# Half of the layer-0 column moves on ScalarE's queue, and two mixer blocks of layer 1 turned by VectorE instead of TensorE

## The reference, cut to what matters

```python
for layer in range(DEPTH):                       # DEPTH = 2
    xn = rmsnorm(h, tok_norm_g[layer])
    if layer % 2 == 0:
        mix, q_mem = deltanet_mixer(...)
    else:
        mix, q_mem = spatial_gating_mixer(...)   # u * sg, 1536 wide
    mo = memory_attention(q_mem, mem_n, w_kv)
    h = h + concatenate([mix, mo]) @ tok_w_out[layer]
    hn = rmsnorm(h, ffn_norm_g[layer])
    h = h + square(relu(hn @ ffn_w1[layer])) @ ffn_w2[layer]
return rmsnorm(h, final_norm_g)
```

## Time and profile before

| | us |
|---|---|
| median of 3 runs | 2287.87 |
| lowest, highest | 2287.43, 2288.89 |
| the profiled execution | 2289.45 |
| its span in the profile | 2287.1 |
| busy time of PE in it | 2267.3 |

### The profile page before, as it was taken

The page is one execution under the profiler, slowest core; times in us unless marked ns, Lnnn a source line. Parts: engine busy times, 40 slices in busy tenths (PEclk is TensorE's granted clock), DMA queues, the critical chain, the costliest instruction groups (busy, mean ns, idle before and its releaser), DMA issues.

```text
span 2287.1 us, 33236 instructions
## 1 busy us (share of the span) xinstructions
PE 2267.3 (99%) x10565; PEld 1889.2 (83%) x10565; DVE 1446.8 (63%) x2465; ACT 1267.9 (55%) x2303; POOL 360.5 (16%) x698
## 2 busy tenths in 40 slices
PE   9999999999999999999999999999999999999997
PEld 7888888888888888888888888888888888888886
DVE  6678788787766555555655655566555555566554
ACT  6566475574456544455554555546565444556544
POOL 0010100000332410013421100021233000242100
PEclk9999999999999999999999999999999999999999
DMA  9655365464577766677766675667777666777665
GB/s 335 182 157 161 114 168 139 137 186 117 172 209 213 219 204 194 195 203 220 218 209 206 203 218 157 167 206 222 211 220 216 198 193 195 212 220 211 204 194 158
DMA packets 253035, 443.84 MB, mean 194 GB/s; under 512 B 38124, under 2 KB 40045, under 8 KB 252781
## 3 DMA queue, kind: packets, MB, share of 16 engines
q1 hardware_dynamic: 231709, 420.15, 62.7%
q0 software_dynamic: 20480, 21.01, 2.8%
q10 hardware_dynamic: 720, 1.06, 0.1%
HBM read 419.00 MB, written 2.10 MB: 184 GB/s over the span
## 4 chain that ended last, share of the span: by engine, by line
PE 93%; DVE 3%; ACT 1%; DMA 1%; issue 1%; POOL 1%; SPq 0%; POOLq 0%; ACTq 0%; DVEq 0%
PE pair L566 29%; PE pair L568 29%; PE pair L567 29%; PE aux L766 3%; PE aux L577 2%; DVE w_lo L1601 1%; DVE r L1946 1%; PE aux L813 0%; DMA raw<-in_dn_w_in 0%; POOL xn_late L2427 0%; DVE attnT L1940 0%; DVE projections L1846 0%; ACT r L1323 0%; PE aux L697 0%; PE aux L714 0%
## 5 line engine op out<-in xcount | busy, mean ns | idle before, releaser
L1601 DVE TENSOR_TENSOR w_lo<-raw,w_hi 128x512 fp32r<-128x512 f32 x1536 | 1025.2, 692 | 640.4 <-ACT w_hi L1064 636.9
L1064 ACT ACTIVATE w_hi<-raw 128x512 fp32r<-128x512 f32 x1536 | 945.7, 633 | 803.4 <-DMA raw<-in_ffn_w 630.4
L566 PE MATMUL pair<-w_hi,xT 128*128 128x512 f32 x1984 | 781.6, 394 | 4.2 <-DVE w_lo L1601 1.9
L568 PE MATMUL pair<-w_hi,xT 128*128 128x512 f32 x1984 | 772.9, 390 | 0.0
L567 PE MATMUL pair<-w_lo,xT 128*128 128x512 f32 x1984 | 772.4, 389 | 0.0
L566 PEld LDWEIGHTS pair<-w_hi,xT 128*128 128x128 f32 x1984 | 372.6, 188 | 84.2 <-issue 3.4
L568 PEld LDWEIGHTS pair<-w_hi,xT 128*128 128x128 f32 x1984 | 372.4, 188 | 78.4
L567 PEld LDWEIGHTS pair<-w_lo,xT 128*128 128x128 f32 x1984 | 372.8, 188 | 74.6
L566 PE MATMUL pair<-w_hi,hid_hi 128*128 128x512 f32 x1012 | 393.8, 389 | 0.1
L568 PE MATMUL pair<-w_hi,hid_lo 128*128 128x512 f32 x1012 | 393.7, 389 | 0.0
L567 PE MATMUL pair<-w_lo,hid_hi 128*128 128x512 f32 x1012 | 393.7, 389 | 0.0
(11 more groups left out here) (255 smaller groups left out, 1164.6 us busy)
## 6 DMA issues: line engine op xcount, KB each, us to landing
raw<-in_ffn_w SPq DMA_DIRECT2D x1024, 256.0 KB, 3.2
raw<-in_dn_w_in SPq DMA_DIRECT2D x208, 256.0 KB, 2.9
raw<-in_tok_w_out SPq DMA_DIRECT2D x128, 256.0 KB, 3.2
raw<-in_gm_w_in SPq DMA_DIRECT2D x112, 256.0 KB, 2.9
xn_late<-xn_late POOLq DMA_DIRECT2D x640, 32.0 KB, 3.0
raw<-in_mem_w_kv SPq DMA_DIRECT2D x64, 256.0 KB, 3.3
r<-in_mem_columns SPq DMA_DIRECT2D x8, 256.0 KB, 5.4
h<-in_x_columns SPq DMA_DIRECT2D x8, 256.0 KB, 5.6
```

Of the source, the lines that this page charges most:

```text
L566: pe.matmul(acc, act_hi[:, kt, tokens], w_hi[:, slot], start=start, stop=False)
L568: mm = pe.matmul(acc, act_lo[:, kt, tokens], w_hi[:, slot], start=False, stop=last and k == 1)
L1064: act.activation(w_hi[:, slot], raw[:, slot], ACT.Copy).then_inc(hi_ready, 1)
L1601: dve.tensor_tensor(w_lo[:, slot], raw[:, slot], w_hi[:, slot].bitcast(F32), ALU.subtract).then_inc(tiles_split, 1)
```

## The change

In layer 0 the 16 transfers of each of the two blocks are shared out: POOL issues those of two rows of squares, ACT those of the other two, from its own queue. ACT has them in `refill` at steps 2 (block 0) and 4 (block 1), each behind a wait for DVE's turning of that block. Pairs 0 to 3 then wait for both halves.

In layer 1 blocks 0 and 1 of `mix` go the second way: DVE turns each right behind its gating (`turn_mix`), POOL issues the 2 x 16 transfers (`move_mixed`), and ACT and DVE read from `xn_late`. PE transposes pairs 4 and 5 alone. In the plan, pairs 2 and 3 stand at steps 6 and 7 instead of 3 and 4.

```diff
-A_FN1 = A_MIX1 + 6
+A_FN1 = A_MIX1 + 2
-MIX_REFILL = ((), (0,), (1,), (2,), (3,), (), (), (), (), (4,), (5,))
+MIX_REFILL = ((), (0,), (1,), (), (), (), (2,), (3,), (), (4,), (5,))
+        turned_mix = lambda n: flat_late[:, 1024 * n:1024 * n + 1024]
+        moved_mix = lambda n: flat_late[:, 1024 * n + 2048:1024 * n + 3072]
+        def move_columns(e, r, n, squares, landed):
+            e.wait_ge(sem("columns_turned"), 2 * sum(MOVED[0:r]) + 2 * n + 2)
+            turned = turned_at(r, n).rearrange("p (a m y) -> p a m y", a=4, m=2)
+            moved = moved_at(r, n).rearrange("p (m b y) -> p b m y", m=2, b=4)
+            for a in squares:
+                for b in range(4):
+                    e.dma_start(moved[32 * a:32 * a + 32, b], turned[32 * b:32 * b + 32, a]
+                                ).then_inc(landed, 16)
...
             def mix_refill(plan):
                 for pairs in plan:
                     for p in pairs:
-                        pe.wait_ge(sem("gated"), 2 * (p // 2) + 2)
-                        pair_transposes(mix_fill[1][p], mix, p)
+                        if p > 3:
+                            pe.wait_ge(sem("gated"), 2 * (p // 2) + 2)
+                            pair_transposes(mix_fill[1][p], mix, p)
             def out_block(n):
                 for s in range(SLABS):
-                    if s < 6:
+                    if s < 4:
+                        pe.wait_ge(sem("mix_split"), s + 1)
+                    elif s < 6:
                         drained(pe, mix_fill[1][s])
...
             def refill(r, gain, plan, ends, slab=None):          # ScalarE
-                for pairs in plan:
+                for step, pairs in enumerate(plan):
+                    if r == 0 and step in (2, 4):
+                        move_columns(act, r, step // 2 - 1, (2, 3), sem(f"columns_moved_too{step // 2 - 1}"))
...
-                            act.wait_ge(sem(f"columns_moved{r}{p // 2}"), 256)
+                            act.wait_ge(sem(f"columns_moved{r}{p // 2}"), 256 if r else 128)
+                            if r == 0:
+                                act.wait_ge(sem(f"columns_moved_too{p // 2}"), 128)
...
                 for pairs in MIX_REFILL[0:8]:                    # ScalarE, out_split
                     for p in pairs:
-                        operand_hi(A_MIX1 + p, p, None)
+                        act.wait_ge(sem(f"mix_moved{p // 2}"), 256)
+                        slab_done(act, 8 * (B_GM + 6) + p)
+                        act.activation(by_square(xT_hi[:, 2 * p:2 * p + 2, :]), mixed_columns(p), ACT.Copy
+                                       ).then_inc(sem("xT_hi_ready"), 2)
...
+            def turn_mix(n):                                     # VectorE
+                for m in range(2):
+                    dve.wait_ge(sem("gated"), 2 * n + m + 1)
+                    dve.transpose(turned_mix(n)..., mix[:, m, n * NB:(n + 1) * NB]...
+                                  ).then_inc(sem("mix_turned"), 1)
             def gating(b):
                 yield
                 gate(b)
+                turn_mix(b)
                 yield
             def out_split():
                 for step, pairs in enumerate(MIX_REFILL):
                     if step == 1:
                         gate(1)
+                        turn_mix(1)
...
                     for p in pairs:
-                        operand_lo(A_MIX1 + p, p, None, 80 + 2 * (p + 1) + 4 * (p > 3))
+                        if p > 3:
+                            operand_lo(mix_fill[1][p], p, None, 84 + 2 * (p + 1))
+                        else:
+                            dve.wait_ge(sem("xT_hi_ready"), 80 + 2 * (p + 1))
+                            high, low = (by_square(x[:, 2 * p:2 * p + 2, :]) for x in (xT_hi, xT_lo))
+                            dve.tensor_tensor(low, mixed_columns(p), high.bitcast(F32), ALU.subtract).then_inc(sem("mix_split"), 1)
...
+            def move_blocks(r):                                  # GpSimd
+                for n in range(MOVED[r]):
+                    move_columns(pool, r, n, range(2 if r == 0 else 4), sem(f"columns_moved{r}{n}"))
+            def move_mixed():
+                for n in range(2):
+                    pool.wait_ge(sem("mix_turned"), 2 * n + 2)
+                    ...                                          # 16 transfers, as in move_columns
-            move_columns(0)
+            move_blocks(0)
             norm(N_FFN0)
             move_hidden(0)
-            move_columns(1)
+            move_blocks(1)
             norm(N_TOK1)
             norm(N_V, MIX)
-            move_columns(2)
+            move_mixed()
+            move_blocks(2)
```

More of the change, by code:

```diff
@@ L326, in encoder_trunk @@
         mix_fill = [[A_MIX0, A_MIX0 + 1, A_MIX0A, A_MIX0A + 1, A_MIX0B, A_MIX0B + 1],
-                    [A_MIX1 + p for p in range(6)]]
+                    {4: A_MIX1, 5: A_MIX1 + 1}]
         refill_slots = [{p: a + p - 2 * n for p in range(2 * n, 8)} for a, n in zip((A_FN0, A_TN1, A_FN1), MOVED)]
@@ L369, in columns_moved, with mixed_columns, by_square @@
             return moved_at(r, p // 2).rearrange("p (x f i) -> p f x i", x=8, f=4)[:, 2 * (p % 2):2 * (p % 2) + 2]
+        def move_columns(e, r, n, squares, landed):
[6 more added lines that the diff above has]
+                                ).then_inc(landed, 16)
+        def mixed_columns(p):
+            return moved_mix(p // 2).rearrange("p (x f i) -> p f x i", x=8, f=4)[:, 2 * (p % 2):2 * (p % 2) + 2]
+        def by_square(t):
+            return t.rearrange("p k (x i) -> p k x i", x=8)
         def freed(ins, n):
@@ L1563, in out_split @@
                     for p in pairs:
-                        operand_hi(A_MIX1 + p, p, None)
+                        operand_hi(mix_fill[1][p], p, None)
                     yield
@@ L2293, in gate @@
                     dve.tensor_tensor(t, t, ug[:, m, b * NB:(b + 1) * NB], ALU.mult).then_inc(sem("gated"), 1)
+            def turn_mix(n):
+                for m in range(2):
+                    dve.wait_ge(sem("gated"), 2 * n + m + 1)
+                    dve.transpose(turned_mix(n).rearrange("p (a m f i) -> p m f a i", a=4, m=2, f=4)[:, m],
+                                  mix[:, m, n * NB:(n + 1) * NB].rearrange("p (f a i) -> p f a i", f=4, a=4)
+                                  ).then_inc(sem("mix_turned"), 1)
             def gating(b):
@@ L2417, in move_hidden @@
                                                    ).then_inc(sem(f"hidden_moved{half}{j}"), 16)
-            def move_columns(r):
+            def move_blocks(r):
                 for n in range(MOVED[r]):
-                    pool.wait_ge(sem("columns_turned"), 2 * sum(MOVED[0:r]) + 2 * n + 2)
-                    turned = turned_at(r, n).rearrange("p (a m y) -> p a m y", a=4, m=2)
-                    moved = moved_at(r, n).rearrange("p (m b y) -> p b m y", m=2, b=4)
+                    move_columns(pool, r, n, range(2 if r == 0 else 4), sem(f"columns_moved{r}{n}"))
+            def move_mixed():
+                for n in range(2):
+                    pool.wait_ge(sem("mix_turned"), 2 * n + 2)
+                    turned = turned_mix(n).rearrange("p (a m y) -> p a m y", a=4, m=2)
+                    moved = moved_mix(n).rearrange("p (m b y) -> p b m y", m=2, b=4)
                     for a in range(4):
@@ L2427, in move_columns @@
                             pool.dma_start(moved[32 * a:32 * a + 32, b], turned[32 * b:32 * b + 32, a]
-                                           ).then_inc(sem(f"columns_moved{r}{n}"), 16)
-            move_columns(0)
+                                           ).then_inc(sem(f"mix_moved{n}"), 16)
+            move_blocks(0)
             norm(N_FFN0)
             move_hidden(0)
-            move_columns(1)
+            move_blocks(1)
             norm(N_TOK1)
             norm(N_V, MIX)
-            move_columns(2)
+            move_mixed()
+            move_blocks(2)
             norm(N_FFN1)
```

## The result

| | before | changed |
|---|---|---|
| median of 18 runs, us | 2287.88 | 2292.0 |
| the profiled execution | 2289.45 | 2291.4 |
| its span | 2287.1 | 2289.6 |

The ratio is 1.0018, with a 95% interval of 1.0011 to 1.0026: 4.1 us slower, 2.5 to 6.0 by the interval. The two profiled executions differ by less, 2.5 us in the span, because that of before lay 1.6 us above its median and that of the changed kernel 0.6 us under its own.

What follows compares the result with a forecast made beforehand. TensorE was taken as the bound, busy 2267.3 of 2287.1 us at top clock. Layer 1's -1.92 and layer 0's +0.42 made -1.5 us, median 2287.87 to 2286.4 us, range 2284.1 to 2288.8.

Steps and rivals of the forecast that it cites:

- c: Layer 0: time from one transfer issue to the next on ScalarE's queue, taken as 0.41 us, between 0.38 and 0.47.
- What the new issues cost: Layer 0 part of the prediction: ScalarE's two runs of eight issues delay the FFN's start to 619.07 us, losing 0.42 us.
- -1.92 - 6.14: Fixed terms of the forecast total for both layers, -1.92 - 6.14 + 16c us; above zero from c = 0.504.
- the formula 612.51 + 16c: Layer 0: time in us at which TensorE's FFN starts, after VectorE's pair 0; 619.07 with c = 0.41, against 618.65 before.
- issue is dear, and the kernel is slower: Rival, chance 0.10: ScalarE between slabs 4 and 7 of `PART_B`; with c at 0.62 the total is +1.9 us, 2289.7 us.
- Slab 7's wait: Layer 0: TensorE would start slab 7 at 613.70 us but get it at 615.3, a new wait of 1.6 us.
- The same recurrence: Layer 0: step-by-step times of ScalarE's issues and splits and VectorE's 0.6 us slots, leading to the FFN's start.
- A1: Layer 0: when ScalarE is free after its first eight issues, 602.85 + 8c us; the split of slab 5 is queued behind.
- Layer 1: Four groups of four TensorE transposes go, 0.48 us each: gain 1.92 us, with nothing late.
- the landing: Layer 1: block 1's last transfer lands at 1483.6 us, needed by 1485.2, with 1.6 us in hand.
- the slack before pair 4: Layer 1: VectorE's gating of block 2 ends 0.26 us ahead of TensorE's transposes of pair 4, instead of 0.86.
- The halves land no sooner: Rival, chance 0.08: split transfers land when the whole did, layer 0 gives and costs nothing; 2286.0 us.

Runs made afterwards that it cites:

- layer 0's half alone: The whole change with everything of layer 1 put back as it was, all six pairs of mix transposed by TensorE: 2294.34 us against 2287.9, ratio 1.0029.
- two other traces: Two versions with layer 0 as before: layer 1's half alone, 2285.79 us, and the same with pairs 2 and 3 at steps 3 and 4, 2292.46 us.
- layer 1's half alone: The whole change without ScalarE's issues, GpSimd issuing all 16 transfers of both layer-0 blocks: 2285.79 us against 2287.9, ratio 0.9991.
- Two delays: The whole change with ScalarE issuing its eight transfers for one layer-0 block only: block 1 only, 2287.29 us against 2288.29; block 0 only, 2287.57 against 2288.1.

## Why the prediction was wrong

- **The step that failed** is the value of c in "What the new issues cost": "I take 0.41, from the row of the same form". It measured 0.66. With it the FFN's start was due at 623.0 us, not 619.07, and layer 0's loss at 4.4 us, not 0.42. The form of the transfer was the wrong likeness; the memories on its two sides were the right one, and no row of the kernel before had both on the chip for this kind of queue. The bounds of 0.38 to 0.47 came from the same rows, so they didn't hold it either. The nearest row by memories was GpSimd's own, 0.53 us from one issue to the next, and it wasn't used; it would have given -1.92 - 6.14 + 8.5 = +0.4 us.
- **The mechanism was right.** With the measured 16c = 10.5 us the formula 612.51 + 16c gives 623.0 us for the end of VectorE's pair 0; the trace has 621.62 + 0.87 + 0.39 = 622.9 us. The sum with it is -1.92 - 6.14 + 10.5 = +2.4 us. That is the rival "issue is dear, and the kernel is slower", with its point of decision at c = 0.504, to which 0.10 was given; its size there, 1.9 us, was still too small.
- **What the sum lacked** is the clock. With 3.04 us of idling at slab 7 the granted clock fell, 1.6 to 1.7 us were lost, a term that the sum put at nothing, and TensorE itself, not pair 0, became last: the FFN starts at 624.0 us on the old clock instead of 623.0. With this 1.0 us the sum is +3.4 us.
- **The base** was one execution. The remaining 0.7 us to the measured 4.1 are inside its interval of 2.5 to 6.0, and they are also the 0.7 us by which 618.65 stood above the start of 617.9 that two other traces show. From 617.9 the sum is -1.92 + (624.0 - 617.9) = +4.2 us, and layer 0's half alone +6.1 where 6.4 was measured. This is likely, not shown: there is one trace of the kernel before. The runs' median was taken from the profiled execution's by a constant, 1.58 us, as if every wait had been the same in both.
- **Waits.** Slab 7's wait was forecast at 1.6 us and came to 3.0. The waits at slabs 5 and 6 (1.2 and 0.6 us) were not forecast. The same recurrence gives the first of them: slab 5's low part is ready at A1 + 1.4 = 604.25 + 8c, with c = 0.66 at 609.5, where TensorE was due at 613.70 - 2 x 2.72 = 608.26. The low part of slab 6 stands behind VectorE's turning of block 1, and so comes late as well.
- **Layer 1** came out as forecast, term by term: 1.92 us forecast, 1.94 in the trace, 2.1 by the medians; the landing to 0.1 us, by two errors that cancel; the slack before pair 4 to 0.01 us.
- **"The halves land no sooner"** fell. With 4 of 16 issues on SyncE, pair 0's high part starts at 614.37 us, against 616.77 before and 615.80 in layer 1's half alone, and the FFN doesn't wait; the issue time was the part worth saving. The Trainium skill's sentence in "DMA: Bandwidth & Descriptors", section "Issuing engines are not separate DMA queues", says that only the sequencer's time is saved, and that it is usually small beside the transfer. On the first the traces agree: GpSimd's transfers of block 0 took 3.1 us to land in the median before, 3.4 with four on SyncE, 3.7 with eight on ScalarE. On the second they agree for one issue of 32 KB, 0.53 to 0.66 us with the gap behind it, but sixteen in a row took GpSimd 8.1 us.

## What to carry to other kernels

Price an issued transfer on the engine that would issue it by a row with the same memories on both sides, not by one of the same shape; if there is none, the range must reach far above the rows. A run of issues on an engine that feeds the bottleneck is a wait for that engine's every customer: spread the issues into gaps that the timeline shows, or give them to a queue that has such gaps. And the waits of TensorE of 3 us here had a second price, since the clock was lower behind them; a wait of 1.6 us had none. A start that hangs on the last of many landings differs from one execution to the next: take it from more than one trace before a forecast is built on it.

## What the runs showed that was not expected

- An issue between two places in on-chip memory took 0.61 to 0.62 us on ScalarE in four shapes, 0.60 on SyncE and 0.54 on GpSimd in one; with the source in device memory 0.44 to 0.45 on ScalarE, and to device memory 0.34.
- The clock fell behind waits of 3.0 us (to 0.55 for 3.7 us) and 4.5 us (to 0.50 for 4 us, then 0.78 for 4 us), and stayed at 1.00 behind waits of 0.2 to 1.6 us, two of them (1.24 and 0.56 us) ending 3.5 us apart.
- Two delays that cost 1.1 and 1.6 us apart, by medians with wide intervals, cost 6.4 together.
